# Laying the experts' third split-weight buffer and the two split rows lower in SBUF, in a two-block transformer with eight experts

## The reference

```python
def swiglu(h, w_gate, w_up, w_down):
    return (jax.nn.silu(h @ w_gate) * (h @ w_up)) @ w_down

def moe_swiglu(h, router, w_gate, w_up, w_down):
    ...
    for e in range(N_EXPERTS):                       # 8 experts, 1024 x 1536 each, top 2 of 8
        out = out + gates[:, e:e + 1] * swiglu(ht, w_gate[e], w_up[e], w_down[e])
```

## Time and profile before

| what | value |
|---|---|
| time, median of 3 runs (lowest to highest) | 1377.47 us (1377.16 to 1379.37) |
| the profiled execution's own time | 1378.74 us |
| its span, first to last instruction | 1376.9 us |
| granted TensorE clock, mean | 0.995 |
| PE busy / DVE busy / ACT busy | 97% / 79% / 62% |
| mean HBM traffic | 220 GB/s over the span |

### The profile page before, as it was taken

How to read it: one execution, slowest core, us unless ns; L and a number is a source line. 1 busy time by engine, 2 the same in 40 slices (tenths; PEclk the granted TensorE clock), 3 DMA queues, 4 the chain that set the end, 5 groups by cost and what they waited for, 6 DMA issues and landing times.

```text
span 1376.9 us, 20551 instructions
## 1 busy us (share of the span) xinstructions
PE 1335.2 (97%) x7374; PEld 1144.0 (83%) x7374; DVE 1094.3 (79%) x1671; ACT 848.5 (62%) x1255; POOL 105.3 (8%) x102
## 2 busy tenths in 40 slices
PE   7999899999999999999999999999999999999999
PEld 7896697888889987898888898887888888888887
DVE  4999666766668877766666797767999999999998
ACT  4557553444436774454444468435888888888886
POOL 0000000000002130000000012200010010110111
PEclk9999999999999999999999999999999999999999
DMA  8652343555554520355565453038999999999997
GB/s 301 209 181 92 123 153 112 168 197 195 185 183 135 171 81 1 125 182 184 189 193 191 140 167 117 1 108 282 393 361 398 380 371 395 380 370 398 382 365 280
DMA packets 149554, 304.25 MB, mean 221 GB/s; under 512 B 7248, under 2 KB 79340, under 8 KB 149356
## 3 DMA queue, kind: packets, MB, share of 16 engines
q1 hardware_dynamic: 146736, 294.76, 60.7%
q0 software_dynamic: 2192, 7.87, 2.4%
q10 hardware_dynamic: 556, 0.67, 0.2%
HBM read 295.93 MB, written 7.34 MB: 220 GB/s over the span
## 4 chain that ended last, share of the span: by engine, by line
PE 81%; DVE 13%; ACT 4%; issue 1%; DMA 0%; SPq 0%; POOL 0%; DVEq 0%; ACTq 0%
PE bank L565 19%; PE bank L567 18%; PE bank L566 18%; PE bank L623 10%; PE bank L625 5%; DVE weights_split L2186 4%; DVE arena L2401 2%; PE bank L1116 1%; PE bank L1122 1%; PE bank L1107 1%; ACT weights_split L1603 1%; PE bank L1134 1%; PE bank L1390 1%; DVE arena L2772 1%; DVE features_split L2265 1%
## 5 line engine op out<-in xcount | busy, mean ns | idle before, releaser
L1603 ACT ACTIVATE weights_split<-weights 128x1024 fp32r<-128x1024 f32 (+4 forms) x266 | 258.4, 1022 | 238.9 <-PE bank L567 152.3
L2186 DVE TENSOR_TENSOR weights_split<-weights,weights_split 128x1024 fp32r<-128x1024 f32 (+4 forms) x258 | 294.9, 1185 | 129.5 <-ACT weights_split L1603 129.3
L565 PE MATMUL bank<-weights_split,features_split 128*128 128x512 f32 (+3 forms) x560 | 216.0, 386 | 3.8 <-DVE weights_split L2186 1.7
L567 PE MATMUL bank<-weights_split,features_split 128*128 128x512 f32 (+3 forms) x560 | 212.0, 379 | 0.0
L566 PE MATMUL bank<-weights_split,features_split 128*128 128x512 f32 (+3 forms) x560 | 211.5, 378 | 0.0
L623 PE MATMUL bank<-features_split,weights_split 128*128 128x512 f32 x560 | 198.4, 399 | 0.3 <-DVE weights_split L2186 0.3
L625 PE MATMUL bank<-features_split,weights_split 128*128 128x256 f32 x560 | 157.3, 281 | 0.0
L565 PE MATMUL bank<-weights_split,hidden_split 128*128 128x512 f32 x376 | 147.9, 393 | 0.0
L567 PE MATMUL bank<-weights_split,hidden_split 128*128 128x512 f32 x376 | 146.6, 390 | 0.0
L566 PE MATMUL bank<-weights_split,hidden_split 128*128 128x512 f32 x376 | 146.5, 390 | 0.0
L623 PEld LDWEIGHTS bank<-features_split,weights_split 128*128 128x128 f32 x560 | 105.2, 188 | 26.5 <-DVE weights_split L2186 0.5
(11 more groups left out here) (423 smaller groups left out, 2534.8 us busy)
## 6 DMA issues: line engine op xcount, KB each, us to landing
weights<-in_moe_gate_dram SPq DMA_DIRECT2D x34, 1024.0 KB, 9.0
weights<-in_moe_down_dram SPq DMA_DIRECT2D x24, 1024.0 KB, 11.2
weights<-in_w_in_dram SPq DMA_DIRECT2D x20, 1024.0 KB, 5.3
weights<-in_w_up_dram SPq DMA_DIRECT2D x16, 1024.0 KB, 5.3
weights<-in_w_down_dram SPq DMA_DIRECT2D x16, 1024.0 KB, 5.0
moe_weights_in_normed<-in_moe_up_dram SPq DMA_DIRECT2D x16, 1024.0 KB, 9.9
moe_weights<-in_moe_up_dram SPq DMA_DIRECT2D x16, 1024.0 KB, 8.9
moe_weights_in_residual<-in_moe_gate_dram SPq DMA_DIRECT2D x16, 1024.0 KB, 8.7
```

Source lines behind the costliest of these rows:

```text
L565: pe.matmul(ps, lhs(0), rhs(0), start=start, stop=False, skip_group_check=shared)
L567: return pe.matmul(ps, lhs(1), rhs(0), start=False, stop=stop, skip_group_check=shared)
L1603: do(act.activation(split_flat(j)[:, 0, part], raw_flat(j)[:, part], ACT.Copy), "hi", j, b)
L2186: do(dve.tensor_tensor(split_flat(j)[:, 1, part], raw_flat(j)[:, part], split_flat(j)[:, 0, part].bitcast(F32), ALU.subtract), "lo", j)
```

## The change

Four tensors of the early stages become parts of one, `wide_and_probs`, of which the room is given back; `moe_weights_split` is declared over it instead of over `arena`, and the room that it had over `arena` is left unused so that what follows stays where it was. `weights_split` is declared ahead of `weights` instead of behind it. No line of any engine's program is touched: each engine has the same instructions in the same order with the same semaphores and counts (only names and line numbers differ).

```diff
         HB = sb("hidden_split", [P, 2, 2048], F32R)
+        NPROBS = 3 * TT * S
+        NSIDE = NWIDE + 2 * NPROBS + 2 * LAYERS * P
+        with nc.sbuf_tensor("wide_and_probs", [P, NSIDE], F32) as SIDE:
+            pass
+        MOE_WS = sb("moe_weights_split", [P, 2, SLOT], F32R)
+        sb("moe_behind_split", [P, NSIDE - 2 * SLOT])
+        WD = SIDE[:, 0:NWIDE]
+        PR, PT = [SIDE[:, NWIDE + i * NPROBS:NWIDE + (i + 1) * NPROBS].rearrange("p (a t n) -> p a t n", a=3, t=TT)
+                  for i in range(2)]
+        PW = SIDE[:, NWIDE + 2 * NPROBS:NSIDE].rearrange("p (l i n) -> p l i n", l=LAYERS, i=2)
+        WS = sb("weights_split", [P, SPLIT, 2, SLOT], F32R)
         W = sb("weights", [P, RING, SLOT])
-        WS = sb("weights_split", [P, SPLIT, 2, SLOT], F32R)
         COL = sb("vector_cols", [P, NCOLS])
-        WD = sb("vector_wide", [P, NWIDE])
-        PR = sb("probs", [P, 3, TT, S])
-        PT = sb("probsT", [P, 3, TT, S])
-        PW = sb("pool_weights", [P, LAYERS, 2, P])
         RT = sb("router", [P, KD_, NE])
...
         MOE_W = [sb("moe_weights_in_residual", [P, SLOT]), sb("moe_weights_in_normed", [P, SLOT])]
-        MOE_WS = sb("moe_weights_split", [P, 2, SLOT], F32R)
+        sb("moe_behind_normed", [P, 2 * SLOT])
         XR = sb("moe_rows", [P, TT, D])
```

## The result

The changed kernel is slower: 1384.36 us median of 7 runs (1384.11 to 1389.73) against 1378.63 us (1377.16 to 1381.77, 7 runs) for the kernel before, ratio 1.0047 with a 95% interval of 1.0032 to 1.0062. The forecast was 1372.7 us, with a range up to 1379.4. The profiled execution of the changed kernel took 1389.73 us, 1387.9 of it span; it is the slowest of its seven, so one profile against the other shows more than the medians do. The granted clock of an execution moves its time too: five of the seven executions of the changed kernel, its median among them, had 0.997 of the full clock, while the kernel before had 0.993 to 0.996 in most of the executions taken beside the experiments. At the same 0.994 the changed kernel took 1388.46 us (one execution) and the kernel before 1379.4 to 1380.2 (eleven), so, clock for clock, the change costs nearer 8.7 us than the 5.7 of the medians.

What follows compares the result with a forecast made beforehand. PE's pace was taken as the bound; 0.60 us saved in each of eight experts is 4.8 us, all else zero, so 1377.47 - 4.8 = 1372.7 us, range 1371.0 to 1379.4 with the slower case left out.

Steps and rivals of the forecast that it cites:

- What bounds the kernel: Whole kernel: PE is the bound, nobody holds it up, and its pace is the expert's time, 52.10 us.
- Third buffer, 0.60 us an expert: Experts: moving `moe_weights_split` from 159808 to 63776 saves 0.60 us each, 4.8 us for eight, settling of `weights_split` included.
- `weights_split` stays inside the flat stretch: zero: Matmuls moving `weights_split`: lying 5984 bytes lower leaves their pace as it was, cost zero.
- the flat stretch: Addresses from 31 to 121 thousand, where the gap between matmuls was taken as flat, against 20.0 ns at 159808 to 176192.
- Height: Main case: a moving operand lying high slows PE's matmuls by 6.7 ns each; chance 0.58, 1371.5 to 1374.7 us.
- the 390-wide slots: Slots with rows at mixed offsets in low addresses: cost 1 ns, not 6.7, taken as speaking against the phase rival.
- Phase instead of height: Rival on split operands: streams run evenly only if starts agree modulo 1024; `weights_split` is spoiled, +14.9, 1392 us; chance 0.18.
- no change: Rival: the third slot's pace hangs on loop place, banks or halves written meanwhile, not address; 1377.5 us, chance 0.24.
- The rule of the Trainium skill: Matmul spacing depends on moving width alone, N/2.4 + 2.5 ns, with no address term; the change would be worth nothing.
- The other terms at zero: Moving raw slots, probabilities, gains and pool weights costs zero: ACT and DVE pace doesn't depend on address, no wait added.
- the 4.7 us in the earlier trace: Experts' stage: ACT's largest single wait for data, in six experts, which could grow by 0.6 us in each.

Runs made afterwards that it cites:

- E1: The changed kernel with `weights_split` 864 bytes higher, at 83232, five small tensors declared ahead of it: 1373.81 us beside 1379.26 for the kernel before, ratio 0.9961.
- E8: The kernel before with `moe_weights_split` 224 bytes higher, at 160032, still over `arena`: 1374.17 us beside 1379.06, ratio 0.9964.
- E4: E1 with only `moe_weights_split` 32 bytes higher, at 63808: 1377.64 us in one execution, beside 1379.26 for the kernel before.
- E2: The changed kernel with `weights` declared ahead of `weights_split` again, which puts `weights_split` at 106944: 1388.27 us, ratio 1.0063 to the kernel before.
- E7: E1 with `features_split`, `hidden_split`, `moe_weights_split` and `weights_split` all 32 bytes higher: 1373.64 us in one execution, beside 1379.06 for the kernel before.
- E12: E9 with the split weights of the stages where activations move 16 bytes lower instead of 32: 1372.59 us in one execution.
- E3: E1 with `features_split`, `hidden_split` and `moe_weights_split` 32 bytes higher, `weights_split` left in place: 1379.22 us, ratio 1.0022 to the kernel before.
- E9: E1 with split weights written and read 32 bytes lower in stages where activations move: 1367.64 us, ratio 0.9917 to the kernel before.

## Why the prediction was wrong

**What bounds the kernel: right.** PE's pace was the time, before and after and in the experiments alike. An expert's length moved with the paces of its two kinds of matmul: 52.08 us before, 52.60 after, 51.48 in E1 (the two sums and 2.16 us of other work, the same in each).

**Third buffer, 0.60 us an expert: right in size, wrong in reason.** E1's expert is 51.48 us, 0.60 less than before, of which 0.405 come from the third buffer's own matmuls (16.961 - 16.556) and 0.195 from those of `weights_split` behind them (32.964 - 32.769). The sum had 0.40 and 0.20. In whole kernels it is 4.9 us in E8 and 5.5 in E1 against 4.8 forecast. But the cause was not that the buffer lay high. E8 leaves it higher than it was and has all of the gain; E4 lays it low with the old relation and has none in the experts' stage. That the 389 ns and the 4.8 us came out as forecast was luck: the new place happens to have relation 0.

**The step that failed: "`weights_split` stays inside the flat stretch: zero".** It was worth 1.02 us an expert: the 144 matmuls take 33.787 us in the changed kernel and 32.769 in E1, 7.1 ns each. With 0.10 us for the third buffer, which now has to settle behind `weights_split` instead of the other way, it is 1.12 x 8 = 8.9 us in the experts. Less the 4.8 won, that leaves 4.1 us more, and the first and last starts above show 3.7 over seven and a half experts. The rest lies ahead of the experts: 1.6 us of the 5.7 by the medians, 4.6 of the 8.7 at the same clock.

**Why the flat stretch misled.** Rows 4, 5 and 7 had three operands with a gap of 13.4 ns, and all three had relation 0 (all start 288 bytes past a multiple of 1024); the one with 20.0 ns had another relation and was also the highest. Height and phase fitted the trace equally well. What tipped the choice were the 390-wide slots, whose rows of weights start at mixed offsets and cost 1 ns. The runs don't overturn that reading, only what was concluded from it: in the changed kernel those matmuls stand 17.0 ns beyond their columns and 396-wide ones 15.4 (15.7 before), so narrow, mixed rows pay at most 2 ns where 512 wide pays 7. It was evidence on another form, and it was given more weight than a form that makes up most of the kernel.

**The rival "Phase instead of height": right in mechanism and sign, its price too high.** It named the offsets (64 mended, 448 spoiled), the sign that would show it (`weights_split` at 396: it is 397), and 1392 us against 1384.36 measured. Its 18.8 us charged all 2808 matmuls with `weights_split` moving. In the experts it was 8.9 us. Ahead of them the starts give, from E1 to the changed kernel: 1272 matmuls 512 wide with weights moving pay 6.2 ns each (7.9 us), the 384 narrower ones (384 to 396 wide) pay -1 to 2 ns, the 1616 with activations moving 256 wide pay 0.5 (0.8 us), and the 560 with activations moving 512 wide win 3.7 each (2.1 us), 6.6 us in all. By medians the two kernels are only 10.5 us apart, which would leave 1.6 for the early part; but E1's median execution had a granted clock of 0.995 and the changed kernel's 0.997. At 0.994 they took 1374.39 and 1388.46 us, 14.1 apart, which leaves 5.2. The profiles fit that: the experts begin 8.9 us later than in E1 (966.1 against 957.2), 2.6 of which are there by the hundredth matmul, where the first window's clock is 0.86 against 1.00, and the window from 25 to 240 us has 0.98 against 0.99, by estimate (0.01 of 215 us) some 2 us more. That leaves about 4. So the early price is 4 to 5 us and a part of the 6.6 did not reach the end of the stage; why was not tried.

**The rival "no change"**, that the pace hangs on the third slot's place in the loop, fell with E1 and E8, which leave the loop alone. The rule of the Trainium skill that went with it, in "TensorE: Matmul & The Clock Gate", section "Back-to-back issue gap", is narrower than the prediction has it: N/2.4 + 2.5 ns is given there for an isolated matmul, and for a stream of weight loads and matmuls the section says that both set the spacing, with about 131 ns at 512 columns. Neither has a term for where the operands lie, and neither is what these traces show: at 512 columns, one clock and one form they have 226.7 to 234.0 ns.

**The other terms at zero were right.** DVE's and ACT's busy time per expert is 48.63 and 43.45 us (48.65 and 43.49 before), with the raw slots 51 thousand bytes higher, and no new wait stands in the list. The probabilities and gains moved in E1 and not in E8, and at a granted clock of 0.994 E1 took 1374.39 us and E8 1374.79 and 1375.1, so their move costs nothing that shows. One row was misread without harm: the 4.7 us in the earlier trace rows are five waits together, the longest 1.3 us, and not a single one.

## What to carry to other kernels

When a change moves operands of a matmul, write down the first byte of both operands before and after, take the difference modulo 256, and treat every pair whose difference changes as repriced; 864 bytes ahead of one buffer moved this kernel by 10.5 us. Here that holds for float32r matmuls; no other type was run. When two causes fit every row of a trace, price both to the end and give them chances accordingly, and don't let a row on another shape decide between them. When medians a few tenths of a per cent apart are compared, put the granted clocks of the executions beside them: two of the differences here change by 3 us or more at the same clock. Before a buffer is moved for its pace, try padding it in place: E8's two lines gave what a rebuilt layout was meant to give.

## What the runs showed of the hardware

- The pace of back-to-back float32r matmuls, 128x512 with a 128*128 load each, at the full clock, depends on where moving and stationary operand start relative to each other. Starts that agree modulo 256 bytes give 226.7 ns, all other relations tried (16, 32, 64, 128, 160, 224) 228.9 to 234.0. Neither height (E2, E4, E8) nor the common start (E7) matters. What in the chip does this was not tried.
- The sign depends on which operand streams and how. Activations moving 512 wide, in turn with 256-wide ones, stand 22.5 ns beyond their columns at relation 0 (E1), 18.8 in the changed kernel, 18.2 in E12, and 15.1 to 15.4 where the split weights lie 32 bytes lower against them (E3, E9). The 256-wide ones out of `features_split` stand at 12.0 ns (E1), 12.5, 12.6 and 10.7 in the same order. That 0 is best can't be carried over to another pattern untested.
- A run that begins behind matmuls of the other relation takes some matmuls to come to its own pace: the third buffer at relation 0 takes 16.556 us an expert behind even ones (E1) and 16.652 behind uneven ones (the changed kernel).
- The granted clock in the first 25 us differs from one execution to the next (0.86, 0.93 and 1.00 in three profiles), which shifts everything behind it by up to 2.6 us. Over a whole execution the means run from 0.990 to 0.999, and the time goes with them: the kernel before took 1375.6 us at 0.998 and 1382.1 at 0.993.
